# A two-block transformer kernel: four rearrangements of weight conversions, modulation loads and the first attention

## What is computed

```python
def swiglu(h, w_gu, w_down):
    g, u = jnp.split(h @ w_gu, 2, axis=-1)
    return (jax.nn.silu(g) * u) @ w_down

def rg_lru(x, w_a, b_a, w_x, b_x, lam):
    r = sigmoid(block_diag_linear(x, w_a, b_a)); i = sigmoid(block_diag_linear(x, w_x, b_x))
    a = exp(-LRU_C * r * softplus(-lam))
    u = sqrt(1 - a**2) * (i * x)
    return associative_scan(h[t] = a[t] * h[t-1] + u[t])

def first_block(x, c, ...):                    # 8 heads of 64, 512 tokens
    mod = (silu(c) @ w_ada + b_ada).reshape(b, 3, 3, 1024)
    x = sandwich(x, swiglu 1, ...)             # "ffn1"
    x = sandwich(x, mixer, ...)                # "mix1": attention, recurrence, gates
    x = sandwich(x, swiglu 2, ...)             # "ffn2"

def second_block(x, c, ctx, ...):              # two layers, each:
    mod_x, mod_c = silu(c) @ w_mod + b_mod, silu(c_ctx) @ w_mod + b_mod
    x = x + gate * norm(token_mixer(...))      # "mix2", "mix3"
    x = x + gate * norm(square(relu(h @ w1)) @ w2)   # "mlp1" (768 tokens), "mlp2" (512)
```

## Time and profile before

| | us |
|---|---|
| median of 3 runs | 4464.09 |
| lowest and highest run | 4456.55, 4465.99 |
| the profiled execution, device time | 4472.22 |
| its span, first to last instruction | 4470.3 |
| mean granted TensorE clock | 0.943 |

### The profile page before, as it was taken

The page is one execution under the profiler, slowest core; times in us unless marked ns, Lnnn a source line. Parts: engine busy times, 40 slices in busy tenths (PEclk is TensorE's granted clock), DMA queues, the critical chain, the costliest instruction groups (busy, mean ns, idle before and its releaser), DMA issues.

```text
span 4470.3 us, 50814 instructions
## 1 busy us (share of the span) xinstructions
PE 3978.6 (89%) x18628; PEld 3190.3 (71%) x18628; DVE 2296.9 (51%) x3495; ACT 1369.7 (31%) x1832; POOL 1350.3 (30%) x1012
## 2 busy tenths in 40 slices
PE   7999787999997888889879979999887979788999
PEld 6888674877776846757758868888674847667887
DVE  4676735126665263452582257777536252834334
ACT  3222533242224242143122242111324243224223
POOL 1444330433443202102232322332220303444443
PEclk8999898999998999999989989999998989999999
DMA  4454210223332101101111123333110201122222
GB/s 175 166 191 160 74 68 29 103 76 132 141 141 85 54 1 39 51 1 38 57 66 48 61 81 113 113 115 120 47 54 0 80 10 66 68 83 76 97 100 85
DMA packets 57219, 364.66 MB, mean 82 GB/s; under 512 B 5744, under 2 KB 12144, under 8 KB 13936
## 3 DMA queue, kind: packets, MB, share of 16 engines
q1 hardware_dynamic: 42064, 271.11, 17.2%
q10 hardware_dynamic: 15008, 91.49, 5.4%
HBM read 360.49 MB, written 2.10 MB: 81 GB/s over the span
## 4 chain that ended last, share of the span: by engine, by line
issue 66%; POOL 23%; PE 10%; DVE 0%; ACT 0%; POOLq 0%; DVEq 0%; ACTq 0%
POOL b_wlo L558 23%; PE ps L1640 3%; PE ps L1641 3%; PE ps L1642 3%; POOLq L572 0%; ACT ps L613 0%; DVE b_y L1151 0%; DVE b_x L1155 0%; PE ps L1692 0%; DVE b_y L1178 0%; PE ps L1703 0%; ACT b_whi L599 0%; POOLq L574 0%; DVE b_y L1204 0%; PE ps L1716 0%
## 5 line engine op out<-in xcount | busy, mean ns | idle before, releaser
L558 POOL TENSOR_TENSOR b_wlo<-b_raw,b_whi 128x512 fp32r<-128x512 f32 x1008 | 1350.1, 1370 | 3099.6 <-ACT b_whi L599 3099.6
L1640 PE MATMUL ps<-b_hhi,b_whi 128*128 128x512 f32 (+1 forms) x3160 | 1185.4, 375 | 110.2 <-POOL b_wlo L558 45.0
L1641 PE MATMUL ps<-b_hlo,b_whi 128*128 128x512 f32 (+1 forms) x3160 | 1169.0, 370 | 0.0
L1642 PE MATMUL ps<-b_hhi,b_wlo 128*128 128x512 f32 (+1 forms) x3160 | 1167.3, 369 | 0.0
L1640 PEld LDWEIGHTS ps<-b_hhi,b_whi 128*128 128x128 f32 x3160 | 607.1, 192 | 220.6 <-issue 65.5
L599 ACT ACTIVATE b_whi<-b_raw 128x2048 fp32r<-128x2048 f32 x252 | 480.7, 1907 | 743.4 <-PE ps L1642 731.4
L1641 PEld LDWEIGHTS ps<-b_hlo,b_whi 128*128 128x128 f32 x3160 | 607.3, 192 | 98.8 <-issue 1.9
L1642 PEld LDWEIGHTS ps<-b_hhi,b_wlo 128*128 128x128 f32 x3160 | 605.4, 192 | 100.3
L1099 DVE SCALAR_TENSOR_TENSOR b_macc<-b_mraw,b_csil,b_macc 128x256 f32<-128x256 f32 x868 | 508.9, 642 | 7.0
L1204 DVE TENSOR_TENSOR b_y<-ps,b_y 128x512 f32<-128x512 f32 x496 | 335.5, 689 | 263.1 <-PE ps L1642 263.0
L1640 PE MATMUL ps<-b_whi,b_dhi 128*128 128x512 f32 x992 | 397.9, 401 | 41.5 <-DVE b_y L1204 23.6
(11 more groups left out here) (277 smaller groups left out, 4770.8 us busy)
## 6 DMA issues: line engine op xcount, KB each, us to landing
b_raw<-panels SPq DMA_DIRECT2D x252, 1024.0 KB, 4.8
b_mraw<-mod_panels ACTq DMA_DIRECT2D x78, 1024.0 KB, 6.6
b_y<-mod_panels ACTq DMA_DIRECT2D x3, 1024.0 KB, 15.9
b_xin<-xT SPq DMA_DIRECT2D x1, 2048.0 KB, 25.5
b_mraw<-mod_panels SPq DMA_DIRECT2D x2, 1024.0 KB, 18.9
b_rope<-rope ACTq DMA_DIRECT2D x4, 512.0 KB, 3.8
outT<-b_xout SPq DMA_DIRECT2D x4, 512.0 KB, 3.8
b_mod<-mod_panels ACTq DMA_DIRECT2D x1, 1024.0 KB, 20.9
```

Of the source, the lines that this page charges most:

```text
L558: ins = pool.tensor_tensor(wlo[:, s, c], raw[:, s, c], whi[:, s, c].bitcast(F32), ALU.subtract)
L1640: pe.matmul(out, a[0], b[0], start=first, stop=False)
L1641: pe.matmul(out, a[0], b[1], start=False, stop=False)
L1642: return pe.matmul(out, a[1], b[0], start=False, stop=last)
```

## The change

Four parts.

1. `first_ups` of the gated stages (ffn1, ffn2) computes half 0 (panel p0) alone in the loop over k, waits only for panel p0's low part, and then computes half 1 (panel p0+1) in one piece.
2. In a recurrent round `split(p+3)` stands behind the two gelus. It was the first thing of the next round. After the fourth round it is the split of the second query panel, which stood behind a wait for the end of the recurrence.
3. `halves_of` shares a chunk's modulation panels between the halves: of two panels the second moves to the head of half 1 (ffn2, mlp1, and two leading chunks of ffn1). Three panels are shared as before.
4. The first attention: a head has three banks for scores and transposes and one of banks 6 and 7 for its output, `pt` has two buffers, and PE weighs head u-1 behind the transposes of head u.

```diff
+    halves_of = lambda n: (range(0, (n + 1) // 2), range((n + 1) // 2, n))
...
             def units(c, p, i=None, mods=(0, 0)):          # on ACT; the same in DVE's units
                 for n in range(2):
-                    for v in (range(2, mods[1]) if n else range(min(2, mods[1]))):
+                    for v in halves_of(mods[1])[n]:
                         mod_load(mods[0] + v, i, 2 * m.half)
...
                     act.activation(gy[:, n, :], ps[:, 2 + n, :], ACT.Gelu_apprx_tanh).then_inc(*up("gelu", (r, n)))
+                split(p + 3)
...
             def first_ups():
-                pe.wait_ge(lo_ready, m.p0 + m.UP)
+                pe.wait_ge(lo_ready, m.p0 + 1)
                 for k in range(KD):
                     pe.wait_ge(*at("h_lo", (pre, k)))
-                    for n in range(2):
+                    for n in range(1 if m.gated else 2):
...
                     turn_more(pre, k)
+                if m.gated:
+                    pe.wait_ge(lo_ready, m.p0 + 2)
+                    for h in range(2):
+                        for k in range(KD):
+                            ins = up_product(m.p0, 1, h, k)
+                    ins.then_inc(panel_used, 1)
...
+    SCORE_ORDER, TURN_ORDER = (2, 0, 1, 3), (1, 3, 0, 2)
+    head_bank = lambda u, w: (3 * (u % 2) + (1, 2, 1, 0)[w - 1], 3 * P if w == 1 else 0)
...
             def weigh(u):
-                b, t = 4 * (u % 2), u // 2
+                b, t = 6 + u % 2, u // 2
...
             for u in range(HEADS):
                 turn(u)
-                weigh(u)
+                if u >= 1:
+                    weigh(u - 1)
                 if u + 2 < HEADS:
                     scores(u + 2)
+            weigh(HEADS - 1)
```

More of the change, by code:

```diff
@@ L811, in keep_transposed @@
             def keep_transposed(u):
-                for j in range(4):
+                for j in TURN_ORDER:
                     act.wait_ge(*at("tr", (u, j)))
-                    if u >= 1:
-                        act.wait_ge(*at("pv", u - 1))
-                    act.activation(pt[:, j, j * P:L], ps[:, 4 * (u % 2) + j, j * P:L], ACT.Copy).then_inc(*up("pt", (u, j)))
+                    if u >= 2:
+                        act.wait_ge(*at("pv", u - 2))
+                    b, c = head_bank(u, 4 - j)
+                    act.activation(pt[:, u % 2, j, j * P:L], ps[:, b, c:c + L - j * P], ACT.Copy).then_inc(*up("pt", (u, j)))
             load_bias(0)
@@ L1361, in mix1 @@
                     one_head(u + 2)
-                keep(u)
+                if u >= 1:
+                    keep(u - 1)
                 if u + 2 < HEADS:
@@ L1365, in mix1 @@
                     normalise(u + 2)
+            keep(HEADS - 1)
             for k in range(KD):
@@ L1910, in scores @@
                 pe.wait_ge(*at("k", u // 2))
[L1911 to L1915, removed]
+                for i in SCORE_ORDER:
+                    b, c = head_bank(u, i + 1)
+                    if i:
+                        claim([b], ("biased", (u, i)))
+                    ins = pe.matmul(ps[:, b, c:c + (i + 1) * P], qm[:, u % 2, i * P:(i + 1) * P], kf[:, u // 2, 0:(i + 1) * P],
+                                    start=True, stop=True)
+                    if i != 2:
+                        ins.then_inc(*up("scores", (u, i)))
+                C.name("scores", (u, 2), *C.labels[("scores", (u, 0))])
             def turn(u):
                 pe.wait_ge(*at("probs", (u, 3)))
-                for j in range(4):
-                    b = 4 * (u % 2) + j
-                    claim([b], ("pt", (u, j)))
+                for j in TURN_ORDER:
+                    b, c = head_bank(u, 4 - j)
+                    if j != 3:
+                        claim([b], ("pt", (u, 3 if j == 1 else j)))
                     for i in range(j, 4):
-                        ins = pe.transpose(ps[:, b, i * P:(i + 1) * P], pr[:, u % 2, i, j * P:(j + 1) * P], const("ident"))
-                    ins.then_inc(*up("tr", (u, j)))
+                        ins = pe.transpose(ps[:, b, c + (i - j) * P:c + (i - j + 1) * P], pr[:, u % 2, i, j * P:(j + 1) * P], const("ident"))
+                    if j != 1:
+                        ins.then_inc(*up("tr", (u, j)))
+                C.name("tr", (u, 1), *C.labels[("tr", (u, 3))])
             def weigh(u):
-                b, t = 4 * (u % 2), u // 2
+                b, t = 6 + u % 2, u // 2
                 claim([b], ("att", u))
```

15 lines of the change are left out of this document (8 added, 7 removed).

## The result

| | us |
|---|---|
| median of 20 runs before, and of 20 runs of the changed kernel | 4463.72, 4470.76 |
| ratio of the changed kernel to the kernel before | 1.0020 (1.0013 to 1.0027) |
| lowest and highest run of the changed kernel | 4463.47, 4476.35 |
| the profiled execution of the changed kernel: device time, span, mean granted clock | 4463.47, 4461.5, 0.948 |

What follows compares the result with a forecast made beforehand. PE, busy 89% of the span, plus its stops and low-clock stretches were taken as the bound. Terms -10.0 - 8.3 + 12 + 1.9 - 28 - 18 + 74 = +23.6 on the median 4464.1 gave 4488 us, range 4456 to 4512.

Steps and rivals of the forecast that it cites:

- stop of 4.3: mlp1: PE stops 4.3 us a chunk for DVE's additions where it stopped 0.65, +3.6 us a chunk before clock.
- behind a longer stop I take four in five: ffn2: the clock falls in four of five chunks behind a new 2.5 us stop, costing 1.35 against 0.8 us.
- I get rounds of 26 to 28, take 27: Recurrent rounds: 27 us against 33.2 on average, with the convolution next in line, 3 x 6.2 = -18.6 us.
- a recurrent round would be PE's 26 us: Recurrent rounds: without the GpSimd-DVE port lock a round takes PE's 26 us, with it 27, 3 us in all.
- the two terms written there, 18.6 and 10: Part 2: -18.6 us from three recurrent rounds and -10 from the stop before the second query panel; together -28.
- The floor of 8.6 a head: First attention: DVE's own work per head sums to 8.6 us, once its wait for the product goes.
- the 0.7 added for PE at the low clock: First attention: 9.3 us a head taken instead of 8.6, as PE at the low clock needs 10.8.
- +4.7 in ffn2: ffn2's first chunk: both modulation loads late, so 42 us against 37.3, +4.7 us.
- (a): Rival: the late modulation loads don't cost; mlp1 -9, ffn2 -25, -98 in all, 4366 us; chance 0.07.
- (c): Rival: recurrent rounds hang on the convolution, DVE meeting POOL throughout; 31 us instead of 27, 4500 us; chance 0.12.
- (d): Rival: clock stays low twice as long behind each mlp1 stop, 2.8 to 3.4 us lost; 4505 to 4512; chance 0.14.
- Rival (b): mlp1 and ffn2 stops cost bare length, clock staying 2.4 GHz; mlp1 +50, ffn2 +1, 4453 us; chance 0.15.

Runs made afterwards that it cites:

- p1_first_products: The kernel before with part 1 alone (first products of ffn1 and ffn2 by halves): 4457.33 us against 4466.02, ratio 0.9981.
- p3_halves: The kernel before with part 3 alone (second of two modulation panels at the head of half 1): 4536.65 us against 4466.02, ratio 1.0163.
- no1_without_first_products: The changed kernel with part 1 undone, parts 2, 3 and 4 kept: 4482.01 us against 4463.35 for the kernel before, ratio 1.0045.
- p2_splits: The kernel before with part 2 alone (next round's second panel split behind the gelus): 4429.77 us against 4466.02, ratio 0.9917.

## Why the prediction was right and wrong

The stops that go and the stops that come were named rightly; three terms make the miss. A recurrent round was put at 27 us, bound by the chain of ACT and DVE, and takes 25.2, PE's own work. The clock behind ffn2's new stop was taken to fall in four chunks of five and fell in one of four. And mlp1 cost 69.5 us for 74. By its own steps:

- **mlp1 held.** Load issued behind the rounded copy, 4.9 us to DVE's start, stop of 4.3: measured 4.9 and 4.1. The chunk was put at 35.9 + 3.6 + 1.7 and is 35.9 + 3.5 + 1.6. +69.5 for +74: the first of the 14 chunks lost 3.2 and not 5.3, the others 5.1.
- **ffn2's mechanism held, its clock did not.** Both stops were forecast in place and length. The step that failed is "behind a longer stop I take four in five": the clock fell in one chunk of four, so a steady chunk costs +0.2 and not +0.8, though it takes 37.3 with the clock up where the forecast had 37.0. Over eight chunks that is 5 of the 6 us by which the term was off (-2.4 for +3.7).
- **Part 2 was mis-sized, the largest miss.** The step is "I get rounds of 26 to 28, take 27", and beside it "a recurrent round would be PE's 26 us". PE's work for two panels is 22.2 us from start to start, where the forecast had 22.9, and the gate matmuls take 3.0: 25.2, and the round is exactly that. PE does not wait for the convolution: ACT's copies to `xpad` and DVE's operations on them lie beside PE's second bank and its panel p+1, and the last is done 0.4 us before PE needs it. -34.9 by the traces and -36.3 by the medians of the part alone, for -28 (the two terms written there, 18.6 and 10, add up to 28.6). A convolution beside POOL takes 5.06 us and alone 2.33, as in the earlier trace rows. But DVE is busy for 21.4 of the round's 25.2 us, and the time that it loses beside POOL, which was to cost 1 us a round, fits into that slack with 0.4 us left. The lock between GpSimd and DVE that the Trainium skill, SBUF — State Buffer, section SBUF: two separate sides, describes fits both durations; the use that the forecast made of it, to speak against part 2, fell.
- **Part 4** gave -21.4 alone (14 to 26 us by its interval's ends, 0.9969 and 0.9942) for -18. The floor of 8.6 a head was the answer (8.7); the 0.7 added for PE at the low clock did not come: the head in which PE's scores took 3.86 us for 2.42 was as long as the others, and PE's next stop was 1.3 us in place of 3.1.
- **Part 1: right in company, wrong as a part.** The stops went, and the low part of the next panel came in time: no stop behind POOL between chunk 0 and chunk 1. The forecast put the new stops of the first chunk under part 3 (+4.7 in ffn2, measured 5.3), so its sum for the chunk, -8.3 + 4.7 = -3.6, fits the measured -2.9. But the reading behind it was wrong: these stops are no price of part 3. Without part 3 they are larger (8.6 and 4.2 us), and p1_first_products, which was expected at -19 by the same reckoning, gave -8.7.

By the traces the touched stages miss the forecast by -2.3 (ffn1), -6.9 (part 2), -2.0 (part 4), -6.1 (ffn2) and -4.5 (mlp1): -21.8. The medians miss it by 16.6. All five lie on the same side, but two of them owe it to the execution of before that was profiled. With the mean of the executions that run a stage's old code (382.0 us in ffn1 from three, 92.3 in the attention from four) ffn1 misses by -1.5 and the attention by +2.0, and the sum is -17. The miss is that of part 2, ffn2 and mlp1. In ffn2 the forecast had gone above the share that the trace showed, four chunks in five for one in two. On terms of -36 to +74 each miss is small; on a remainder of +24 together they are 70%. The rivals stay apart: (a) is refuted by 37 DMA waits, (c) by rounds of 25.2, (d) by chunks of 41.0. Rival (b), that the clock stays up, came true in ffn2 for the most part and in mlp1 not at all. Its 4453 assumed both.

**What stays open.** The two profiled executions give +1.8 for the touched stages and the medians +7.0. The attention of before explains 4 of the difference, if the mean of the four traces with the old order is taken for it (96.3, 91.6, 87.8, 93.5: 92.3). Also open is part 1's own price: 8.7 us by the medians and some 3.5 by the traces. The argument on the attention is drawn from four executions and is not a test. It was not tried what decides whether the clock falls behind a stop of 2 us.

## What to carry to other kernels

A load issued by a compute engine leaves when that engine's program reaches it: moving a consumer's work later in a loop doesn't ask for the load to move too, and a load placed behind a wait arrives one round trip late each time. When a stop is removed, look at the engines that kept pace while it lasted: their work now lags and stands in the way somewhere else, and what the edit is worth depends on the order of their programs. Where large terms nearly cancel, size each one against the bare work of the engine that will bound it, for two or three small misses of the same sign become most of the answer.

## What the runs showed of the hardware

The granted clock differs between identical pieces of work. Behind the same 1.8 us stop of ffn2, chunks of before take 36.7 or 38.3 us, about by turns. Behind a stop of 2.4 us, five microseconds later in the chunk, it fell in two chunks of eight (in one of eight in p3_halves and in no1_without_first_products); behind 4.1 us in mlp1 in all thirteen steady ones; behind 0.6 to 0.8 us in none. The same happens to whole stages: the old attention in the kernel before and in p2_splits, which leaves it untouched (windows, columns as above),

```profile
676.00:772.30 96.30, 62.85 (x211) 39.94 (x210) 57.68 (x149) 33.52 (x98) 0.00 (x0) 0.79 0.04 12
```

```profile
636.00:723.80 87.80, 53.38 (x210) 34.38 (x210) 57.52 (x149) 33.41 (x98) 0.00 (x0) 0.90 0.04 13
```

has the same DVE and ACT work and 8.5 us between them: a mean clock of 0.79 against 0.90, which is 1.2 GHz for 0.21 x 2 x 96 = 40 or for 0.10 x 2 x 88 = 18 us of the stretch. In a chain that goes back and forth between PE and DVE, one pair of traces can't price an edit to better than that. Neither can the difference of two profiled spans when the sum is 7 us: here it had the other sign than the medians.
